# No gathered row while the gate maps are made, and other places for the kept-map passes

## What is computed

```python
def peer_mixer(h, wq, subkeys, u, v):
    q = (h @ wq).reshape(B, S, 8, 2, 128)
    scores = einsum('bshcd,hcnd->bshcn', q, subkeys)      # two scores over 128 keys
    s_top, i_top = top_k(scores, 16)
    cand = s_top[..., 0, :, None] + s_top[..., 1, None, :]
    cand_idx = i_top[..., 0, :, None] * 128 + i_top[..., 1, None, :]
    best, pos = top_k(cand.reshape(..., 256), 16)
    expert_idx = take_along_axis(cand_idx, pos)
    gates = softmax(best)
    # per token, over its 128 picks:
    a = einsum('cd,ced->ce', h, u[expert_idx])
    act = gelu(a) * gates
    return einsum('ce,ced->cd', act, v[expert_idx])
```

## Time and profile before

| | us |
|---|---|
| runs, median of 3 | 3875.9 (3874.65 to 3895.38) |
| profiled execution | 3852.57 |
| its span | 3850.8 |
| PE busy | 3490.0 (91%) |
| DVE busy | 2636.5 (68%) |
| ACT busy | 982.7 (26%) |
| POOL busy | 1382.5 (36%) |

### The profile page before, as it was taken

How to read it: one execution, slowest core, us unless ns; L and a number is a source line. 1 busy time by engine, 2 the same in 40 slices (tenths; PEclk the granted TensorE clock), 3 DMA queues, 4 the chain that set the end, 5 groups by cost and what they waited for, 6 DMA issues and landing times.

```text
span 3850.8 us, 50373 instructions
## 1 busy us (share of the span) xinstructions
PE 3490.0 (91%) x13726; PEld 2235.0 (58%) x13726; DVE 2636.5 (68%) x5617; ACT 982.7 (26%) x2147; POOL 1382.5 (36%) x1220
## 2 busy tenths in 40 slices
PE   4998998999956999999978989989997689999997
PEld 2554445776754448874445544467767544688643
DVE  6656016898898777677566640289899987777774
ACT  1433102322263003330023330123323610133200
POOL 0000002444424565566400000044454256566662
PEclk9999999999978999999989989999998889999999
DMA  6322215888756999899942322178877589999997
GB/s 239 140 103 77 98 61 188 322 311 313 275 180 241 404 401 390 330 388 388 374 183 104 109 85 90 61 260 331 313 286 260 180 306 401 402 377 337 390 392 296
DMA packets 274015, 999.71 MB, mean 260 GB/s; under 512 B 31353, under 2 KB 48249, under 8 KB 262785
## 3 DMA queue, kind: packets, MB, share of 16 engines
q0 software_dynamic: 153600, 553.72, 38.2%
q1 hardware_dynamic: 120194, 443.42, 30.5%
HBM read 971.85 MB, written 25.17 MB: 259 GB/s over the span
## 4 chain that ended last, share of the span: by engine, by line
PE 65%; DVE 22%; issue 4%; DVEq 4%; DMA 3%; ACT 2%; ACTq 0%; POOL 0%; SPq 0%; POOLq 0%
PE ps L605 23%; PE ps L558 12%; PE ps L785 9%; DVE mod L1431 4%; DVE arena L1425 4%; PE ps L516 3%; PE ps L548 3%; PE ps L613 3%; PE ps L493 2%; DMA arena<-in_u_dram,idx 2%; PE ps L636 1%; DVE mod L1445 1%; PE ps L525 1%; PE ps L589 1%; DVE arena L1321 1%
## 5 line engine op out<-in xcount | busy, mean ns | idle before, releaser
L1167 POOL DMA_INDIRECT arena<-in_u_dram,idx x512 | 656.1, 1281 | 984.7 <-issue 652.3
L558 PE MATMUL ps<-hT,mod 128*128 128x256 f32 x4096 | 929.0, 381 | 0.0
L605 PE MATMUL ps<-arena 128*128 128x512 f32 x2048 | 881.5, 594 | 3.7 <-ACT hT L963 3.7
L1167 POOL DMA_INDIRECT arena<-in_v_dram,idx x512 | 630.2, 1231 | 632.2 <-DVE mod L1431 369.6
L558 PEld LDWEIGHTS ps<-hT,mod 128*128 128x128 f32 x4096 | 762.4, 191 | 92.1
L1425 DVE CUSTOM_DVE_ANT_0 arena<-arena 128x1024 f32<-128x1024 f32 x512 | 617.1, 1226 | 232.7 <-DMA arena<-in_u_dram,idx 229.5
L1431 DVE SCALAR_TENSOR_TENSOR mod<-arena,mod 128x1024 f32<-128x1024 f32 x512 | 657.3, 1284 | 121.4 <-DMA arena<-in_v_dram,idx 91.6
L605 PEld LDWEIGHTS ps<-arena 128*128 128x128 f32 x2048 | 390.4, 191 | 492.3 <-issue 492.2
L979 ACT COPY mod<-ps 128x512 f32<-128x512 f32 x512 | 274.6, 590 | 553.2 <-PE ps L548 553.2
L548 PE MATMUL ps<-const,arena 128*128 128x128 f32 x2048 | 269.1, 275 | 17.8 <-ACT mod L979 16.6
L548 PEld LDWEIGHTS ps<-const,arena 128*128 128x128 f32 x2048 | 239.0, 141 | 49.1 <-ACT mod L979 23.9
(11 more groups left out here) (202 smaller groups left out, 3477.2 us busy)
## 6 DMA issues: line engine op xcount, KB each, us to landing
arena<-in_u_dram SPq DMA_DIRECT2D x256, 512.0 KB, 6.9
arena<-in_v_dram SPq DMA_DIRECT2D x256, 512.0 KB, 6.8
arena<-in_ada_w_dram SPq DMA_DIRECT2D x56, 1024.0 KB, 4.9
arena<-in_w_qkv_dram SPq DMA_DIRECT2D x48, 512.0 KB, 5.6
arena<-in_w_m_dram SPq DMA_DIRECT2D x16, 1536.0 KB, 6.6
arena<-in_w_q_dram SPq DMA_DIRECT2D x32, 576.0 KB, 6.3
gate_scratch<-hT SPq DMA_DIRECT2D x64, 256.0 KB, 2.2
hT<-gate_scratch POOLq DMA_DIRECT2D x128, 128.0 KB, 8.1
```

The source lines that it names most:

```text
L558: last = pe.matmul(ps[:, 6 + tile // 2 % 2, tile % 2 * NT:(tile % 2 + 1) * NT], u_turned[:, tile % 2, k * P:(k + 1) * P], hT[:, k, DT0:SEQ ...
L605: last = pe.matmul(ps[:, 2 * c + n, :], act_t[:, e, c * P:(c + 1) * P], stream[:, slot, n * 512:(n + 1) * 512], start=(half == 0 and e == ...
L1167: pool.indirect_dma_start(out=ring[:, r % RING, :], out_offset=None, in_=table, in_offset=bass.IndirectOffsetOnAxis(ap=idx[:, j % 4, k:k + ...
```

## The change

- In the map stage VectorE takes no row. Before it come rows 0 to 160 (before: to 163), behind it rows from 161 (before: in it 164 to 195). The search at row 192 so leaves the stage.
- On ScalarE unit 5 (`unit_gates(l, 5)`) moves from the 17th batch of the stage to behind it.
- The kept-map passes start at rows 336 and 400, not 368 and 432. GpSimd's reads move with them, since both use `KEEP0` and `KEEP1`.
- For head 7 VectorE makes both dense searches first, then takes rows 140 to 147, then the last product of gates, then rows 148 to 160.
- The act tiles of half 0 stand differently between the heads: behind heads 5 and 6 four each, not eight behind head 5. SyncE's loads follow this order (`ENDS`).

```diff
 KEPT = 4
-KEEP0 = 16 * 23
-KEEP1 = 16 * 27
+ENDS = [0, 8, 16, 24, 32, 40, 44, 48]
+G_ROW = 161
+G_END = 161
+KEEP0 = 16 * 21
+KEEP1 = 16 * 25
...
-                for hd in range(HEADS - 2):
+                for hd in range(HEADS - 1):
                     load_q(hd + 1)
-                    more_u(8 * hd + 4, 8)
-                load_q(HEADS - 1)
-                more_u(HALF - 12, 12)
+                    first = STREAM + ENDS[hd]
+                    more_u(first, (STREAM + ENDS[hd + 1] if hd < HEADS - 2 else HALF) - first)
...
-                    if hd < HEADS - 2:
-                        act_tiles(l, 0, 8 * hd, 8 * hd + 8)
-                act_tiles(l, 0, 8 * (HEADS - 2), HALF)
+                    if hd < HEADS - 1:
+                        act_tiles(l, 0, ENDS[hd], ENDS[hd + 1])
+                act_tiles(l, 0, ENDS[-1], HALF)
...
-                    if b == 16:
-                        unit_gates(l, 5)
                 keep_batch(l, NB - 1)
-                for j in range(6, 9):
+                for j in range(5, 9):
                     unit_gates(l, j)
...
-            def gate_maps(l, row0):
+            def gate_maps(l):
...
                         gate_batch(l, b - 1)
-                    rows(l, row0 + b, row0 + b + 1)
                 gate_batch(l, NB - 1)
...
-                for hd in range(HEADS):
+                for hd in range(HEADS - 1):
                     rows(l, 20 * hd, 20 * hd + 10)
                     topk_dense(l, hd, 0)
...
+                topk_dense(l, HEADS - 1, 0)
+                topk_dense(l, HEADS - 1, 1)
+                rows(l, 20 * (HEADS - 1), 20 * (HEADS - 1) + 8)
                 gates_dense(l, BLOCKS - 1).then_inc(S["pre_done"], 1)
-                rows(l, 160, 164)
+                rows(l, 20 * (HEADS - 1) + 8, G_ROW)
                 dve.wait_ge(S["pq_ev"], ND * l + ND)
                 park()
-                gate_maps(l, 164)
-                rows(l, 196, KEEP0)
+                gate_maps(l)
+                rows(l, G_END, KEEP0)
```

More of the change, by code:

```diff
@@ L999, in channel_mix @@
                         unit_gates(l, (1, 2, 4, 5, 7).index(hd))
-                    if hd < HEADS - 2:
-                        for tile in range(8 * hd, 8 * hd + 8):
+                    if hd < HEADS - 1:
+                        for tile in range(ENDS[hd], ENDS[hd + 1]):
                             act_tile(l, 0, tile)
-                for tile in range(8 * (HEADS - 2), HALF):
+                for tile in range(ENDS[-1], HALF):
                     if tile == HALF - 4:
```

## The result

The changed kernel takes **3938.99 us** (median of 4 runs, 3925.82 to 3943.15); the kernel before took 3875.28 in the same session (3855.01 to 3895.38). The ratio is **1.0152**, interval 1.0116 to 1.0189: slower by 1.5%. The forecast was 3945.

A forecast was written before the change was run, and what follows sets the result against it. TensorE was taken to bound each layer from the first value product (S), VectorE the map stage before it. Per layer 82.5 us lost after S less 48 won gives +34.5, both +69 on 3875.9: 3945, bounds 3905 to 3970, range 3885 to 3990.

The forecast's parts named there:

- The map stage: Stage before the first value product shrinks from 153.0 to 107 us, bounds 98 and 120, with 40% at 1.2 GHz.
- rival C: TensorE stays at 1.2 GHz in the map stage: 120 us, +13 a layer, 3971 in all; chance 18%.
- The small price of unit 5: ScalarE's unit 5 in the map stage: about 3.2 us, two table loads of 1.28 included; 2 taken as VectorE's gain.
- The start of the stage: VectorE starts the map stage 2 us sooner, bounds 0 and 6.
- The swap of the two gaps: Before the map stage TensorE's 6.79 us gap for head 7's weights becomes about 5 us waiting on a search; the second goes.
- Tile 5: Act tiles, unit 9 before tile 4 waits on ScalarE for row 287: TensorE stalls 13 us, or 11 if rows speed up.
- Tile 34: Act tiles, unit 11 before tile 33 waits for row 351 behind the first kept pass: 29 us stall, bounds 24 and 33.
- Tile 49: Act tiles, unit 12 before tile 48 waits for row 383: late by about 5 us, counted as 6.
- The clock: TensorE at the low clock after its gaps: some 5 us after unit 9's stall, 6 after unit 11's.
- rival A: Faster: ScalarE's waits cost nothing as rows come sooner; -15.5 us per layer, 3845 in all; chance 10%.
- The tail: Rows left after the v stream take 37 us (DMA 39, VectorE 31); layer ends at S' + 801, 24 after TensorE.
- rival B: No change: only tile 33 stalls, 24 us, without clock loss; -0.5 us per layer, 3875 in all; chance 12%.

The follow-up runs named there:

- run 6: Changed kernel with unit 5 put back into batch 16 of the map stage; 3937.92 us, ratio 1.0189.
- run 5: Kernel before with only the act tile order (ENDS) and head 7's search in one piece; 3888.73 us, ratio 1.0047.
- run 7: Changed kernel with one gathered row back in each of the first 31 map-stage batches; 3968.01 us, ratio 1.0257.
- runs 10 and 11: Changed kernel with kept passes at rows 336 and 416 (3880.17 us, 1.0053), and at rows 352 and 416 (3845.86 us, 0.9967).
- runs 1 to 5 and 8: Changed kernel, units late: all 0.9878, first two 1.0083, last two 0.9983; passes at 368/432: 0.9862; both repairs 0.9895. Fifth: kernel before, new order only, 1.0047.
- run 4: Changed kernel with the kept-map passes back at rows 368 and 432, units as in it; 3843.18 us, ratio 0.9862.
- run 9: Changed kernel with the first kept-map pass at row 352 instead of 336, the second still at 400; 3877.79 us, ratio 1.0050.
- runs 1 to 4: Changed kernel with ScalarE's units 9 to 12 later (all 0.9878, first two 1.0083, last two 0.9983); fourth, kept passes back at rows 368 and 432, 0.9862.
- runs 5 to 8: Kernel before with new order only 1.0047; changed kernel with unit 5 back in stage 1.0189, rows back in stage 1.0257, units late and passes at 368/432 0.9895.
- runs 9 to 12: Changed kernel with kept passes at rows 352/400 (1.0050), 336/416 (1.0053), 352/416 (0.9967), and 352/416 with units late (0.9930).
- run 12: Changed kernel with kept passes at rows 352 and 416, units 9 to 11 at tiles 9, 24, 44, unit 12 behind the loop; 3830.83 us, ratio 0.9930.

## Why the prediction was right

Point by point, by its own terms; its working is above.

**The map stage** was taken at 107, bounds 98 and 120; it is 101.8. The batch of 3.02 us was right and is what every batch takes. The share at 1.2 GHz was wrong: I had carried over the 0.79 of the earlier trace rows, but those slow batches went with the rows, and after a first batch of 3.75 TensorE ran at 2.4 GHz, mean clock 0.97. This is 5 us a layer on the fast side, and it rules out rival C. The small price of unit 5 was right as ScalarE's 3.2; run 6 puts the whole at 4.4, and the Trainium skill ("ScalarE: Activation LUTs", What ACT_TABLE_LOAD costs), with 2.66 us a switch, would have made it over 5: the trace has 1.28 between one function and the next here too.

**The start of the stage** was taken 2 us sooner; it is 4.0 and 0.0 later in the changed kernel, 3.5 later in run 5. The swap of the two gaps came as told: 7.08 us at 953.61 (1.80 in layer 1, forecast 5), where ScalarE's Exp waits 8.62 for the search, and no gap of 7 us at the head of the last tiles. But the prediction let hardly anything of it reach the stage, and that was wrong: start and gap are late together. The start less TensorE's gap there is 428.7 and 429.6 us in the changed kernel, and 427 to 432 in the 24 layers of the twelve kernels that have both the new order and 161 rows ahead of the stage, while the start alone goes from 428 to 437. Gap and start both hang on VectorE, whose search the Exp waits for; why it comes up to 9 us late in some layers is open.

**The stalls.** Tile 5: 13 by the sum, measured 13.6 and 13.4; the 127 rows take 257.5 us to 1427.8, not 254. Tile 34: 29, measured 28.4 and 27.5. Tile 49: about 5, measured 8.1 in both layers. The clock: 12 by the sum; 59.6 less the three gaps of 50.1 and the small one of 1.8 leaves 7.7 in layer 0, and 62.6 less 49.0 and 6.0 leaves 7.6 in layer 1. Sum 59, measured 59.6 and 62.6; second pass at 557, measured 557.7 and 562.4. That the sum fits to 1 us is luck: the gaps came 3 us longer, the clock 4 us cheaper, and the small gap was no term. But the two large terms are right each by itself. That tile 34 would stall "at any speed" of the rows, which the prediction held against rival A, is what run 7 shows, and it is the line that I had forgotten when I wrote that run's expectation.

**The tail** is the term that was mis-sized. The second pass opens at 558.7 and its last batch is at 645.6, as told. Then 801 was forecast for the last row, and it is 810 and 815. The stream ended where it should (the last v tile is asked for at 1934.7, forecast S' + 764 = 1934.3) with some 25 rows left, forecast 23. I had set two bounds side by side, 39 us of DMA and 31 of VectorE, and taken 37. Here they came one behind the other. SyncE's issues, and the piece of the chain of waits that follows:

```profile
1882.89 51.86 SPq L386 DMA_DIRECT2D arena<-in_v_dram  x16
1935.10 0.34 SPq L441 DMA_DIRECT2D mod<-mod_scratch  x1
...
1936.60 0.33 SPq L446 DMA_DIRECT2D x_res<-x_scratch  x1
```

```profile
1935.16 19.81 DMA arena<-in_v_dram,idx
```

x and the tables (3.7 MB) are asked for at 1935.1 to 1936.9, and beside them the rows land late until 1955: seven in 20.7 us. The last 18 then run back to back in 25.4 us, bound by VectorE: none waits for its transfer, though GpSimd asks for ten of them only after 1957, as slots of the ring come free. Together 46 us; layer 1 shows the same two parts. The page of the Trainium skill that lets HBM bind near 358 GB/s ("DMA: Bandwidth & Descriptors", Where 436 GB/s comes from) does not explain the 9 us: by it the transfers would take an estimated 44 us, but the engines moved 412 GB/s from 1934 to 1955, and 388 over the 221 us of the first value pass. That x and the tables are what makes the rows late is read from the order of the issues; no run moved them.

Measured by what is queued behind the second pass, from its opening to the last row: 80 rows 251 us (changed kernel), 64 rows 229 to 231 (runs 10 and 11), 48 rows 188 (before).

**The sum.** Per layer +34.5 was forecast and +44.7 measured on the two profiles: 5 less for the stage, then 6 or 2 more for the start (2 sooner was forecast), 1 or 5 for the stalls, 8 for the tail (counted from the second pass). The median came out 6 us under the forecast, which is luck: the kernel before usually runs slower than in its profile, the changed one does not. I had added the difference of the profile to the median of the runs; here that hid 20 us by which the two profiles lie further apart than the sum of the terms. Rival A is ruled out by the gaps, rival B too (its second pass at 522).

## What to carry to other kernels

When work moves from in front of a barrier to behind it in one queue, go through every other queue that waits for that work by number, and ask at each place whether the item it wants now lies behind something that waits for it in turn; such a pair stalls however early the rows come, and one constant can undo it (16 rows, a gap of 28 us a layer). Time freed on one engine is kept only as far as the next chain lies below: here it was 21 us, and it took a re-placing of every due time to keep 8 to 17 of the 51. Forecast a tail piece by piece, first what waits for transfers and then what is left as arithmetic, and not as the larger of the two. And before two profiles are set against each other, see whether they come from the same chip.

## What was not expected of the hardware

- The clock in the map stage: TensorE idles 0.96 us of every 3.01 us batch and has a granted clock of 0.97 over the stage (2.4 GHz but for its first batches), while with a row in each batch (run 7: 4.16 us with a u row, 2.14 of it idle, 4.50 and 2.48 with a v row) it is 0.81. Behind a single wait of 4.20 us one batch of 3.56 stands for 2.05 (run 6). In the waits of 13.6 and 28.4 us the clock falls to 1.2 GHz while TensorE still waits, and is back at 2.4 GHz 4.9 and 3.4 us after it has started again.
- Small gaps on TensorE in the act tiles, 2 to 11 us, in the changed kernel and runs 1 to 5 and 8. In run 4 those without a releaser sum to 30 us beside the gap at tile 5. They aren't u tiles that land late: the tile in question is already turned, and it is ScalarE's copy of it (L981) that comes late, with no other work of ScalarE before it in the profile. Run 4, TensorE and ScalarE, a tile turned by 1493.5 and copied at 1502.08:

```profile
1492.48 1.04 PE L550 MATMUL ps<-const,arena 128*128 128x128 f32 x8
1493.35 3.62 PE L560 MATMUL ps<-hT,mod 128*128 128x256 f32 x16
1502.72 1.12 PE L550 MATMUL ps<-const,arena 128*128 128x128 f32 x4 [5.75 <-issue]
```

```profile
1489.80 0.58 ACT L981 COPY mod<-ps 128x512 f32<-128x512 f32 x1 [0.21 <-PE ps L550]
1502.08 0.58 ACT L981 COPY mod<-ps 128x512 f32<-128x512 f32 x1 [11.70 <-issue]
```

- These late copies go with the chip, or with the session on it, and not with the kernel: run 9 differs from the changed kernel in one constant and has none. A copy that starts more than 1.5 us after its half tile is turned and ScalarE is free occurs 12 times among the 512 of the changed kernel's trace, 13 to 26 times in runs 1 to 4, 6 to 18 times in runs 5 to 8, and never in runs 9 to 12 nor in the kernel before, whose profiled time (3852.57) stands in the record among the runs of the chip of runs 9 to 12. Full DMA engines alone don't bring them: over the act tiles of layer 0 the DMA share is 0.97 in run 4 and 0.99 in run 12. What holds ScalarE up is open. It adds 1.8 and 6.0 us of gaps to the act tiles of the changed kernel, and more to several of runs 1 to 4 and 8, so their wholes stand a little high beside those of the kernel before.
- The kernel before differs by 1% from chip to chip: medians 3897.25, 3867.34 and 3857.47 beside runs 1 to 4, 5 to 8 and 9 to 12, where the third chip is the one without late copies. Whether they are the whole of that difference is open, since the kernel before has a trace from one chip only.
